# A 13-row V ring, U and V rows gathered in turn, and scores two rows earlier in a PEER layer

## The reference, cut to what matters

```python
q = (h @ w_peer_q).reshape(B, S, 8, 2, 128)               # 8 heads, two halves
s = einsum('bshcd,hcnd->bshcn', q, peer_sub_keys)         # 128 keys per half
top_s, top_i = top_k(s, 16)                               # in each half
cand = top_s[..., 0, :, None] + top_s[..., 1, None, :]    # 16 x 16 sums
best_s, best_pos = top_k(cand, 16);  g = softmax(best_s)  # 16 experts per token and head
u = peer_u[idx]; a = gelu(einsum('td,ted->te', h, u))     # rows of 1024 floats
p = einsum('te,ted->td', g * a, peer_v[idx])
x = layernorm(alpha * x + (1 + gate2) * p) * ln2_g + ln2_b
```

## Time and profile before

| | before |
|---|---|
| three runs, us | 998.52, 1005.27, 1005.81 |
| median | 1005.27 |
| the profiled execution | 1007.17, span 1005.4 |
| busy: PE, DVE, ACT, POOL | 79%, 60%, 19%, 49% |
| mean granted TensorE clock | 0.90 |
| HBM read | 336.87 MB, 336 GB/s over the span |
| gathers | 512, first at 250.3 us, last at 987.5 us |

### The profile page before, as it was taken

One profiled execution on the slowest core, in us unless ns is written; L12 is line 12 of the kernel. 1 busy time (PEld: TensorE's weight loads), 2 busy tenths in 40 slices (PEclk: granted clock), 3 DMA queues, 4 the chain that ended last, 5 costly groups with the idle time before them and its releaser, 6 DMA issues.

```text
span 1005.4 us, 8411 instructions
## 1 busy us (share of the span) xinstructions
PE 796.7 (79%) x2726; PEld 463.6 (46%) x2726; DVE 605.9 (60%) x1359; ACT 192.4 (19%) x483; POOL 491.5 (49%) x529
## 2 busy tenths in 40 slices
PE   5999999999694769777696969696676859595764
PEld 5877588867352435334342524243333425252321
DVE  6245675236777575747557474848474665778455
ACT  1012122201313121213022112212120312212111
POOL 1000000000767566756666666666566666666662
PEclk9999999999797979988887979797988879797988
DMA  9998956582999999999999999999999999999994
GB/s 350 375 365 317 343 188 247 196 265 84 341 359 380 328 373 376 376 353 372 347 367 353 366 370 360 376 363 368 365 373 345 358 361 362 368 365 396 358 410 152
DMA packets 112282, 338.48 MB, mean 337 GB/s; under 512 B 9184, under 2 KB 20976, under 8 KB 112112
## 3 DMA queue, kind: packets, MB, share of 16 engines
q0 software_dynamic: 73728, 268.47, 70.9%
q1 hardware_dynamic: 35936, 67.11, 18.7%
q10 hardware_dynamic: 2576, 2.37, 0.8%
HBM read 336.87 MB, written 1.05 MB: 336 GB/s over the span
## 4 chain that ended last, share of the span: by engine, by line
POOL 36%; PE 29%; issue 18%; DVE 7%; another core or an unknown queue 6%; DMA 3%; ACT 1%; POOLq 0%; DVEq 0%; ACTq 0%
POOL ring L351 36%; PE bank L987 10%; PE bank L1159 6%; DVE ring L832 3%; PE bank L1090 3%; PE bank L980 3%; DMA ring<-in_peer_u_dram,small 1%; PE bank L1104 1%; PE h_ps L936 1%; PE bank L1123 1%; PE h_ps L953 1%; PE h_ps L941 1%; DMA ring<-in_peer_v_dram,small 1%; DMA x_sb<-in_x_dram 0%
## 5 line engine op out<-in xcount | busy, mean ns | idle before, releaser
L832 DVE CUSTOM_DVE_ANT_0 ring<-ring,h_ps 128x1024 f32<-128x1024 f32 x256 | 310.9, 1221 | 225.0 <-DMA ring<-in_peer_u_dram,small 203.4
L351 POOL DMA_INDIRECT ring<-in_peer_u_dram,small x256 | 247.5, 967 | 283.7 <-DVE small L813 203.5
L1159 PE MATMUL bank<-ring,small 128*128 128x512 f32 x512 | 258.4, 669 | 150.9 <-ACT small L519 87.2
L351 POOL DMA_INDIRECT ring<-in_peer_v_dram,small x256 | 240.0, 938 | 170.3 <-remote 89.0
L1159 PEld LDWEIGHTS bank<-ring,small 128*128 128x128 f32 x512 | 109.3, 217 | 290.5 <-issue 290.5
L1159 PE MATMUL bank<-ring,h_sb 128*128 128x512 f32 x500 | 225.1, 608 | 16.4 <-ACT h_sb L519 6.5
L1159 PEld LDWEIGHTS bank<-ring,h_sb 128*128 128x128 f32 x500 | 96.5, 196 | 135.5 <-issue 128.5
L987 PE MATMUL bank<-hT,ring 128*128 128x256 f32 x448 | 102.3, 389 | 1.1 <-ACT hT L402 1.1
L987 PEld LDWEIGHTS bank<-hT,ring 128*128 128x128 f32 x448 | 86.3, 194 | 16.3 <-issue 4.4
L1123 PE MATMUL bank<-hT,wpq 128*128 128x128 f32 x512 | 67.9, 288 | 17.6 <-issue 17.1
L1123 PEld LDWEIGHTS bank<-hT,wpq 128*128 128x128 f32 x512 | 65.1, 202 | 27.0 <-issue 26.4
(11 more groups left out here) (159 smaller groups left out, 515.8 us busy)
## 6 DMA issues: line engine op xcount, KB each, us to landing
ring<-in_w_cond_dram SPq DMA_DIRECT2D x10, 2048.0 KB, 13.8
ring<-in_w_in_dram SPq DMA_DIRECT2D x8, 2048.0 KB, 12.3
wpq<-in_w_peer_q_dram SPq DMA_DIRECT2D x8, 1024.0 KB, 12.0
ring<-in_w_cond_dram SPq DMA_DIRECT2D x4, 1024.0 KB, 14.5
ring<-in_w_out_dram SPq DMA_DIRECT2D x2, 2048.0 KB, 10.7
ring<-in_peer_u_dram,small POOLq DMA_INDIRECT x256
ring<-in_peer_v_dram,small POOLq DMA_INDIRECT x256
ring<-in_w_in_dram SPq DMA_DIRECT2D x2, 1024.0 KB, 13.5
```

What stands on the lines that cost most here:

```text
L351: nc.gpsimd.indirect_dma_start(out=dst[e], out_offset=None, in_=table[0], in_offset=bass.IndirectOffsetOnAxis(ap=idx[:, k:k + 1], axis=0)) ...
L832: V.tensor_tensor_reduce(u_ring[e], u_ring[e], h_ps[:], 1.0, 0.0, ALU.mult, ALU.add, acol[:, g, e:e + 1]).then_inc(dots_done, 1)
L1159: last = T.matmul(bank[ACC_BANKS[t][m]][:], diag_of(p, g)[:, e, :], v_ring[e][:, m * BLK:(m + 1) * BLK], start=False, stop=end, skip_group ...
```

## The change

The V ring gets 13 rows. Its first 8 are those of before; the other five are the space of `ln1` (2 rows) and of `cond`'s rows GT1, SH2 and SC2 (3 rows), which the second LayerNorm of tile 1 reads last. Groups 0 and 1 still use 8 slots, later groups go round through 13; `V_SLOT`, `V_TURN` and `V_BEFORE` tabulate slot, turn and predecessor of each of the 256 V rows. GpSimd issues U row e of group n and V row e of group n - 1 in turn. Before every second U row it waits for the two dots of the group before that free the slots, and before every second V row for the two predecessors' use; V row 0 of group 2 also waits for the second LayerNorm of tile 1. The indices get a third buffer. TensorE's scores of pair p + 2 move from before the first row of pair p + 1 to between the sixth and seventh row of the second group of pair p.

```diff
+VROWS_LATER = GROUP + 5
+V_SLOT = [j % GROUP if j < 2 * GROUP else (j - GROUP) % VROWS_LATER for j in range(V_ROWS)]
+V_TURN = [V_SLOT[:j].count(V_SLOT[j]) for j in range(V_ROWS)]
+V_BEFORE = [max((i for i in range(j) if V_SLOT[i] == V_SLOT[j]), default=-1) for j in range(V_ROWS)]
...
-        idx = small[:, 2870:2902].bitcast(U32)
+        idx = small[:, 2870:2918].bitcast(U32)
...
+        v_ring += [ln1[:, 0, :], ln1[:, 1, :], cond[:, GT1, :], cond[:, SH2, :], cond[:, SC2, :]]
...
-                pool.wait_ge(idx_ready, p + 1)
-                for g in range(2):
-                    n = 2 * p + g
-                    first = a * TOPK + g * GROUP
-
-                    pool.wait_ge(dots_done, GROUP * n + GROUP)
-                    for e in range(GROUP):
-                        gather(peer_u, u_ring, e, first + e, u_in)
-                    for e in range(GROUP):
-                        if e % 2 == 0:
-                            pool.wait_ge(v_used, GROUP * n + e + 2)
-                        gather(peer_v, v_ring, e, first + e, v_in)
...
+            def u_row(n, e):
+
+                if e == 0 and n % 2 == 0:
+                    pool.wait_ge(idx_ready, n // 2 + 1)
+                if n == 0:
+                    if e == 0:
+                        pool.wait_ge(dots_done, GROUP)
+                elif e % 2 == 0:
+                    pool.wait_ge(dots_done, GROUP * n + e + 2)
+                gather(peer_u, u_ring[e], n, e, u_in[e])
+
+            def v_row(n, e):
+
+                j = GROUP * n + e
+                if e % 2 == 0:
+                    before = max(V_BEFORE[j], V_BEFORE[j + 1])
+                    pool.wait_ge(v_used, GROUP + max(before + 1, 0))
+                if j == 2 * GROUP:
+                    pool.wait_ge(h2_ready, 2 * TILES)
+                gather(peer_v, v_ring[V_SLOT[j]], n, e, v_in[V_SLOT[j]])
+
+            for n in range(2 * PAIRS + 1):
+                for e in range(GROUP):
+                    if n < 2 * PAIRS:
+                        u_row(n, e)
+                    if n:
+                        v_row(n - 1, e)
...
-                if not (isinstance(p, int) and p == 0):
-
-                    dve.wait_ge(v_used, p * TOPK - TOPK + GROUP)
+                if p >= 3:
+
+                    dve.wait_ge(v_used, GROUP + (p - 2) * TOPK)
...
-                if p + 1 < PAIRS:
-                    score(p + 1)
+                if p == 0:
+                    score(1)
...
+                        if (g, e) == (1, GROUP - 2) and p + 2 < PAIRS:
+                            score(p + 2)
+                        j = GROUP * n + e
+                        pe.wait_ge(v_in[V_SLOT[j]], 16 * (V_TURN[j] + 1))
```

More of the change, by code:

```diff
@@ L196, in build @@
         u_in = [sem(f"u_in{i}") for i in range(GROUP)]
-        v_in = [sem(f"v_in{i}") for i in range(GROUP)]
+        v_in = [sem(f"v_in{i}") for i in range(VROWS_LATER)]
         out_stored = sem("out_stored")
@@ L368, in _, with gather @@
-            for i in range(0, PAIRS // 2):
-                gather_pair(i, 0)
-                gather_pair(i, 1)
+            def gather(table, dst, n, e, landed):
+                p = n // 2
+                k = p % 3 * TOPK + n % 2 * GROUP + e
+                nc.gpsimd.indirect_dma_start(
+                    out=dst, out_offset=None, in_=table[0],
+                    in_offset=bass.IndirectOffsetOnAxis(ap=idx[:, k:k + 1], axis=0)).then_inc(landed, 16)
+            def u_row(n, e):
[7 more added lines that the diff above has]
+                gather(peer_u, u_ring[e], n, e, u_in[e])
@@ L809, in topk_sums @@
                 assert step.n == TOPK_STEPS, step.n
-                if not (isinstance(p, int) and p == 0):
-                    dve.wait_ge(v_used, p * TOPK - TOPK + GROUP)
-                V.scalar_tensor_tensor(out=idx[:, a * TOPK:(a + 1) * TOPK], in0=sel[:, 0:TOPK], scalar=float(NKEYS),
+                if p >= 3:
+                    dve.wait_ge(v_used, GROUP + (p - 2) * TOPK)
+                V.scalar_tensor_tensor(out=idx[:, p % 3 * TOPK:(p % 3 + 1) * TOPK], in0=sel[:, 0:TOPK], scalar=float(NKEYS),
                                        in1=sel[:, TOPK:2 * TOPK], op0=ALU.mult, op1=ALU.add).then_inc(idx_ready, 1)
@@ L861, in own_rows @@
                 for e in DVE_ROWS:
-                    dve.wait_ge(v_in[e], 16 * (n + 1))
+                    j = GROUP * n + e
+                    dve.wait_ge(v_in[V_SLOT[j]], 16 * (V_TURN[j] + 1))
                     if e == DVE_ROWS[0]:
-                        link(V.tensor_scalar(base, v_ring[e], wts[:, 1, e:e + 1], None, ALU.mult))
+                        link(V.tensor_scalar(base, v_ring[V_SLOT[j]], wts[:, 1, e:e + 1], None, ALU.mult))
                     else:
-                        link(V.scalar_tensor_tensor(out=base, in0=v_ring[e], scalar=wts[:, 1, e:e + 1], in1=base,
+                        link(V.scalar_tensor_tensor(out=base, in0=v_ring[V_SLOT[j]], scalar=wts[:, 1, e:e + 1], in1=base,
                                                     op0=ALU.mult, op1=ALU.add))
@@ L1154, in add_rows @@
                     for i, e in enumerate(rows):
-                        pe.wait_ge(v_in[e], 16 * (n + 1))
+                        if (g, e) == (1, GROUP - 2) and p + 2 < PAIRS:
+                            score(p + 2)
+                        j = GROUP * n + e
+                        pe.wait_ge(v_in[V_SLOT[j]], 16 * (V_TURN[j] + 1))
                         pe.wait_ge(diag_ready, GROUP * n + i + 1)
@@ L1158, in add_rows @@
                         for m in range(2):
-                            last = T.matmul(bank[ACC_BANKS[t][m]][:], diag_of(p, g)[:, e, :], v_ring[e][:, m * BLK:(m + 1) * BLK],
+                            last = T.matmul(bank[ACC_BANKS[t][m]][:], diag_of(p, g)[:, e, :], v_ring[V_SLOT[j]][:, m * BLK:(m + 1) * BLK],
                                             start=False, stop=end, skip_group_check=True)
```

7 lines of the change are left out of this document (1 added, 6 removed).

## The result

The changed kernel takes 1067.32 us (median of 4 runs, 1056.7 to 1071.6), beside 1004.92 for the kernel before (median of four now, one run more than the three shown above): 1.062 times, 95% interval 1.0525 to 1.0715. The prediction was 926 us, faster. It was wrong by 141 us and in sign.

A forecast was written before the change was run, and what follows sets the result against it. The prediction took GpSimd as the bound, by its issue pace plus one V-row wait per group. It summed 308 + 471 x 1.273 + 17.9 = 925.5 us of span, 926 us as median; range 908 to 964, 8 in 10.

The forecast's parts named there:

- GpSimd is the bound: its issue pace plus one wait: Expert stage: 16 gathers at 1.24 to 1.25 us plus one V-row wait of some 3.3 us make a 23.2 us group.
- A release that late is a fact of this trace that I can't explain; I carry it as a delay: V-row wait in each group: row through by about 530.6, GpSimd went on at 542.7, 12 us later; kept as a delay.
- Row price 1.273 us: Gathered rows without the wait: one lands every 1.273 us at 412 GB/s, so a pair of groups costs 40.8 us.
- Start (308) and end (17.9): Unchanged ends of the span: 308 us until 472 rows are left, 17.9 us from the last gather to the end.
- TensorE's 32.2 us a pair: TensorE's work for a pair of groups at 2.4 GHz: 32.2 us of the 40.8 available.
- Issue in turn: Alternating U and V rows: waits for U rows cost nothing while the 3.8 us of spare time holds.
- Scores between rows 6 and 7: Scores' new place on TensorE: likely 1.9 us late, against 5.3 at the old place; worth nothing by itself.
- the cover of 3.8: Spare time on VectorE: two dots end at 16.6 us of their group's time, U(n+2,0) wants them at 20.4.
- Rival A: Scores stay late, arriving at 31.8, and VectorE sets the pace: 2.6 us beyond the cover, 962 us; chance 0.13.
- Rival D: Transfers limit at 366 GB/s, or V ring still waits, releases coming later than 24 us; 1000 to 1005 us; chance 0.07.
- B: TensorE's clock swings, at 1.2 GHz half of the time: a pair takes 42.9 us, 957 us in all; chance 0.12.
- C: TensorE's clock is low most of the time; at a mean grant of 0.60, 1116 us, slower; chance 0.05.

The follow-up runs named there:

- v_by_sp: Changed kernel, but from group 4 on SyncE copies 128 consecutive rows where GpSimd gathered V rows; 968.56 us, one run.
- pace2: Changed kernel with a 128-column GpSimd memset, waited for, behind each gather from group 2 on; 1015.56 us, ratio 1.0118.
- scoreback: Changed kernel with the scores back at their old place, behind the eighth V row; 1137.29 us, ratio 1.1225.
- half: Changed kernel with each gather fetching only the first 512 of the 1024 columns of each row; 1077.8 us, one run.
- burst_v13: Changed kernel with the old issue order, eight U rows then eight V rows, keeping 13 V slots and the scores' new place; 1092.54 us, ratio 1.081.

## Why the prediction was wrong

- **"GpSimd is the bound: its issue pace plus one wait"**: right as a sum, 471 times the mean spacing fits both kernels. But the wait wasn't a cost beside the pace: it paid back what the pace of 1.24 had overdrawn. A gather costs about 1.42 us over a longer stretch, and 308 + 471 x 1.42 + 18 = 995 is an estimate of the least that 512 gathers by GpSimd allow in this kernel, 1% under what before has (981, or 2.4%, by the 1.39 of the bursts). No run came near it, so there was little or nothing to win.
- **"A release that late is a fact of this trace that I can't explain; I carry it as a delay"** is the step that failed. The delay was used three times as a constant (12 us in the V ring, 4.4 and 7.9 in the scores). It was an effect of GpSimd's series, which the change made longer. Series of 25 gathers took the query's signal from 5 us to 25 late, and the rows went 1.587 us apart instead of 1.273: 471 x 0.314 = 148 us, which is the whole miss.
- **Row price 1.273 us**: right for the transfers. v_by_sp ran pairs of 41.0 us where the sum had 40.8, at 407 GB/s. The Trainium skill, "DMA: Bandwidth & Descriptors", section "Where 436 GB/s comes from", has the HBM side at about 358; this core, with the others idle, held 407 over 500 us, so the measurement decides against it here. But as a pace for gathers 1.273 was wrong, and the trace of before had the sign of it at the very place where the price was read. The window of 953 to 973 us lies within the longest unbroken series there, 30 gathers from 938.40 to 974.40. TensorE worked through a group in it, from 961.18 on, and all of its recorded signals but one (976.6) came in one burst at 980.8 to 981.1, 6.4 us after the last gather, with GpSimd waiting:

```profile
961.18 15.96 PE L1159 MATMUL bank<-ring,small 128*128 128x512 f32 x32 [9.33 <-issue]
```

```profile
981.10 0.94 POOL L351 DMA_INDIRECT ring<-in_peer_v_dram,small  x1 [5.76 <-remote]
```

- **Start (308) and end (17.9)**: the sums with them come within 4 us of the span in both kernels. **TensorE's 32.2 us a pair**: the pairs of 41.0 us in v_by_sp leave room for no error above 0.2. **Issue in turn** v_by_sp doesn't test, since GpSimd gathers one table there; in pace2, where both leave in turn and nothing hangs, the mean spacing is 1.46 beside neighbours of 1.43, so its waits cost about 1 us a pair.
- **Scores between rows 6 and 7**: priced at nothing by itself; it is worth some 60 us (scoreback) once TensorE crawls. Its sum for the old place is off: with rows 2.55 us apart the scores come at 19.1 + 6.2 + 1.7 + 0.6 + 0.4 + 4.4 = 32.4, 7.0 us after they are wanted, not 5.3. Both eat the cover of 3.8, so nothing changes. A's 31.8 lacks the same 0.6 of the scores' matmuls.
- **Rival A** (scores late, signals bunch until the last row is through) had the mechanism, but priced it at 2.6 us a pair; by the mean spacing a pair took 32 x 1.59 = 50.8 us, 10 more than the forecast's 40.8. **Rival D** had "releases come later than 24 us" and was right in that, but gave 1000 to 1005. **Rivals B and C**: the clock fell, 0.87 to 0.81 in the window above, after TensorE had stood idle between single matmuls. The low clock came second: the crawl began while it still stood at 1.00 (508 to 510). In pace2 it was 0.98 with TensorE waiting some 0.65 to 0.80 us for each row. The Trainium skill, "TensorE: Matmul & The Clock Gate", section "HAM oscillation — how this bites in real kernels", tells of a kernel that waits about 3 to 5 us for a transfer in each step. The waits of this kernel are far shorter, so the prediction was wrong to count that section for B.

Open: what the backlog is. The gathers' packets keep their distance (half), so it isn't their transfers. The Trainium skill, "Perfetto Trace Analysis", section "DMA Instruction — SWDGE (GPSIMD)", says that the profiler ends such an instruction when its last descriptor has been written; what GpSimd still does for a gather beyond that point no run here shows. Why TensorE crawls as well, beyond that its own signals hang, wasn't tried. How far VectorE's own signals hang was seen only in passing, up to 6.8 us in burst_v13.

## What to carry to other kernels

A delay in a trace that nobody can explain isn't a constant: ask what it grows with before building on it, and what else an apparent stall releases. Here gathers by GpSimd 1.24 us apart are an overdraft: above one in about 1.42 us TensorE's signals come late, by up to 25 us in a series of 25. Pauses and pacing free the signals but cost as much as they give: the best of the paced kernels is at 1.011. So count gathers, not bytes, don't lengthen their series, and where rows needn't be gathered, let another queue copy them.

## What the runs showed of the hardware

- Signals of TensorE hang while GpSimd issues indirect gathers in a long series: 24.6 us with series of 25 at 1.24 us, 0.8 us at 1.43. VectorE's were seen late by 6.8 us (burst_v13); landings of U rows came through. Half of the bytes (24.7) or half of the rows (25.8) change nothing; SyncE's copies in place of half of the gathers, at 407 GB/s, do no harm (0.4).
- The burst comes 3.85 us after the last gather of 14, 6.0 after 28.
- With half rows a gather's first data packet starts 1.8 us after its issue and the last has landed after 3.4, at the start of a series as at its end.
- A memset of one column on GpSimd between two gathers costs nothing (1.24 us stays), a waited one 0.08, one of 128 columns 0.19.
- A gather of 64 partitions is issued in 0.90 us, one of 128 in 0.94.
